# An output product in split precision, loads reordered, and three stage starts prepared by the stage ahead

## The reference

```python
def mixer_sublayer(x, mem, w_in, w_mem_kv, w_out, main_fn):
    h = x @ w_in
    ...
    y_main = main_fn(u_main)
    y_mem = memory_attention(q_mem, mem, w_mem_kv)
    y = jnp.concatenate([y_main * jax.nn.silu(g_main), y_mem * jax.nn.silu(g_mem)], axis=-1)
    return y @ w_out
...
        x = layer_norm(ALPHA * x + y, ln_g[layer], ln_b[layer])
...
        y_a = _gmlp_mixer(zu, zv, ...)
        y_b = _rwkv7_mixer(zr, ...)
        y = jnp.concatenate([y_a, y_b], axis=-1) @ w_out[l]
        x = x + gate1[:, None, :] * y
        h = _modulate(_rmsnorm(x, norm2_g[l]), shift2, scale2)
        y = _hier_moe(h, router_group_w[l], router_group_b[l], router_expert_w[l],
                      router_expert_b[l], moe_w_gate[l], moe_w_up[l], moe_w_down[l])
```

## Time and profile before

| | |
|---|---|
| Median of 3 runs | 3203.99 us (3201.82 to 3207.22) |
| The profiled execution | 3200.6 us, span of the trace 3198.9 us |
| Granted TensorE clock, mean | 0.942 |
| TensorE busy | 2877.6 us, 90% of the span |
| VectorE, ScalarE, GpSimd busy | 1745.5, 1076.3, 440.4 us |
| Second output stage | 1410.6 to about 1601 us |
| Mixing stage | 2189.1 to 2455.7 us |

### The profile page before, as it was taken

The page is one execution under the profiler, slowest core; times in us unless marked ns, Lnnn a source line. Parts: engine busy times, 40 slices in busy tenths (PEclk is TensorE's granted clock), DMA queues, the critical chain, the costliest instruction groups (busy, mean ns, idle before and its releaser), DMA issues. The chain is left out here.

```text
span 3198.9 us, 46062 instructions
## 1 busy us (share of the span) xinstructions
PE 2877.6 (90%) x18692; PEld 2100.5 (66%) x18692; DVE 1745.5 (55%) x2741; ACT 1076.3 (34%) x1682; POOL 440.4 (14%) x352
## 2 busy tenths in 40 slices
PE   7999899898999999989889999995796799999991
PEld 5877644576777777754436767684675577777770
DVE  2223323484565666633324625352674799999984
ACT  2111100122444444531221313221243366666652
POOL 1322000021332222300021101011200000000001
PEclk9999999999999999989999999996697799999995
DMA  4111031563212112121121201017433799999985
GB/s 155 50 37 42 7 132 53 182 202 106 66 54 60 53 54 60 54 112 46 40 58 30 67 26 58 7 59 242 144 114 145 254 397 398 398 396 398 399 305 223
DMA packets 290854, 454.34 MB, mean 142 GB/s; under 512 B 15680, under 2 KB 157504, under 8 KB 290672
## 3 DMA queue, kind: packets, MB, share of 16 engines
q1 hardware_dynamic: 283616, 426.05, 38.0%
q0 software_dynamic: 7056, 25.69, 2.0%
HBM read 389.77 MB, written 61.93 MB: 141 GB/s over the span
## 5 line engine op out<-in xcount | busy, mean ns | idle before, releaser
L662 PE MATMUL psum<-wo,yT 128*128 128x512 f32 x768 | 336.3, 598 | 14.6 <-DMA wo<-in_w_out 14.6
L662 PEld LDWEIGHTS psum<-wo,yT 128*128 128x128 f32 x768 | 146.5, 192 | 195.1 <-issue 179.5
L922 PE MATMUL psum<-x_hi,w_hi 128*128 128x512 f32 x512 | 211.4, 413 | 10.2 <-POOL w_lo L1023 10.2
L1112 DVE TENSOR_TENSOR fox_pT_lo<-psum,fox_pT_hi 128x512 fp32r<-128x512 f32 (+2 forms) x192 | 107.1, 558 | 184.8 <-ACT fox_pT_hi L1051 175.7
L924 PE MATMUL psum<-x_hi,w_lo 128*128 128x512 f32 x512 | 201.7, 394 | 0.0
L923 PE MATMUL psum<-x_lo,w_hi 128*128 128x512 f32 x512 | 200.7, 392 | 0.0
L2874 ACT CAST hi_d<-land_d 128x2048 fp32r<-128x2048 f32 x66 | 122.8, 1909 | 140.1 <-PE psum L2746 140.1
L1603 PE MATMUL psum<-hT,wr 128*128 128x512 f32 x384 | 167.1, 593 | 0.0
L162 PE MATMUL psum<-x_hi,w_hi 128*128 128x512 f32 x384 | 152.7, 398 | 9.0 <-POOL w_lo L153 9.0
L3019 DVE TENSOR_TENSOR lo_d<-land_d,hi_d 128x2048 fp32r<-128x2048 f32 x66 | 148.3, 2289 | 21.5 <-ACT hi_d L2874 21.5
L164 PE MATMUL psum<-x_hi,w_lo 128*128 128x512 f32 x384 | 151.2, 394 | 0.0
(11 more groups left out here) (493 smaller groups left out, 6498.4 us busy)
## 6 DMA issues: line engine op xcount, KB each, us to landing
land_g<-in_moe_w_gate SPq DMA_DIRECT2D x66, 1024.0 KB, 7.6
land_u<-in_moe_w_up SPq DMA_DIRECT2D x66, 1024.0 KB, 7.2
land_d<-in_moe_w_down SPq DMA_DIRECT2D x66, 1024.0 KB, 9.0
ada<-in_ada_w SPq DMA_DIRECT2D x24, 1024.0 KB, 5.4
y_slots<-yb SPq DMA_DIRECT2D x33, 512.0 KB, 10.0
w<-in_w_in SPq DMA_DIRECT2D x24, 512.0 KB
wo<-in_w_out SPq DMA_DIRECT2D x12, 1024.0 KB
w_land<-in_w_in SPq DMA_DIRECT2D x24, 512.0 KB, 3.8
```

Of the source, the lines that this page charges most:

```text
L662: last = nc.tensor.matmul(banks[hf][:], E.yT[:, c, t * P:(t + 1) * P], wo[:, c, hf * HALF:(hf + 1) * HALF], start=(c == 0), stop=(c == NY ...
L922: nc.tensor.matmul(bank[:], hi[:, d, :], E.x_hi[:, d, cols], start=(d == 0), stop=False)
```

## The change

Six parts.

1. `stage_out` gets a parameter `whole`. In layer 1 it is 2: chunks 0 and 1 stay f32 matmuls, chunks 2 to 11 become three f32r matmuls each. ScalarE casts ten chunks of w_out, VectorE subtracts them; for each tile GpSimd casts and subtracts y (128x1280). `wo_lo` and `y_lo` take the place of `wo` and `yT` in memory. Two x tiles instead of three. Layer 0 keeps f32.
2. The first two key blocks of the memory stage of layer 1 are loaded by SyncE at the end of layer 0's `stage_out`, into tiles that both stages share. The memory stage in turn loads and splits the first q and the first k block of the fox stage at its end, behind the last `ada` load. `stage_fox` starts with `FIRST = 2` blocks present.
3. In `tail(c)` of the RWKV stage `fill_("GH", c)` moves from behind both heads' GH to between the two, on TensorE and on ScalarE. The four router loads move into this stage's start, waited for at its end.
4. The mixing stage loads by first use; the waits for small operands are split up; the transposes of `ws` follow the first two chains; the zeros are written in five parts, issued in the steps t = 8 to 12 behind the stores of these steps.
5. The casts of `w_o` go from GpSimd to ScalarE, in step t = 2 in front of the copies of tile 0's y; GpSimd keeps the eight subtractions.
6. In the routing preamble the eight small operations for the two weights move behind the first block's `e_x_lo`; TensorE makes the first eight of the table's products when the first choice is placed; two subtractions of expert weights move in front of the wait for the table.

```diff
-def stage_out(nc, E, A, layer, rows_in, rows_out, modulate=False):
+def stage_out(nc, E, A, layer, rows_in, rows_out, modulate=False, whole=NY):
...
+        SPLIT = NY - whole
+        with ExitStack() as raw:
+            wo = E.sb("wo" + n, [P, NY, D], ctx=raw)
+        wo_lo = E.sb("wo_lo" + n, [P, NY, D], F32R, ctx=st)
+        if SPLIT:
+            wo_hi = E.sb("wo_hi" + n, [P, SPLIT, D], F32R, ctx=st)
+            y_hi = [E.sb(f"y_hi{n}_{i}", [P, SPLIT, P], F32R, ctx=st) for i in range(2)]
...
-        NX = 3
+        NX = 2 if SPLIT else 3
...
+                        if t == 0 and c >= whole:
+                            pe.wait_ge(wo_split, c - whole + 1)
+                        if c == whole:
+                            pe.wait_ge(y_split, t + 1)
...
+                            if c < whole:
+                                last = nc.tensor.matmul(banks[hf][:], E.yT[:, c, t * P:(t + 1) * P], wo[:, c, cols], start=first, stop=final)
+                            else:
+                                hi, w_hi = y_hi[t % 2][:, c - whole, :], wo_hi[:, c - whole, cols]
+                                nc.tensor.matmul(banks[hf][:], hi, w_hi, start=first, stop=False)
+                                nc.tensor.matmul(banks[hf][:], hi, wo_lo[:, c, cols], start=False, stop=False)
+                                last = nc.tensor.matmul(banks[hf][:], E.y_lo[:, c, t * P:(t + 1) * P], w_hi, start=False, stop=final)
...
+                if layer == 0:
+                    wkv = A["w_mem_kv"][1].rearrange("(c p) n -> p c n", p=P)
+                    for i in range(2):
+                        sp.dma_start(E.w1[i][:], wkv[:, :, i * P:(i + 1) * P]).then_inc(E.w1_landed[i], 16)
...
+            def _(pool):
+                for t in range(NT if SPLIT else 0):
+                    cols = slice(t * P, (t + 1) * P)
+                    if t >= 2:
+                        pool.wait_ge(ringD.full, ringD.nth(("y", t - 2, 1)))
+                    nc.gpsimd.tensor_copy(y_hi[t % 2][:], E.yT[:, whole:NY, cols]).then_inc(y_hi_set, 1)
+                    pool.wait_ge(y_hi_set, t + 1)
+                    nc.gpsimd.tensor_tensor(E.y_lo[:, whole:NY, cols], E.yT[:, whole:NY, cols], y_hi[t % 2][:].bitcast(F32),
+                                            ALU.subtract).then_inc(y_split, 1)
...
+                for c in range(whole, NY):
+                    if c % 2 == 0 or c == whole:
+                        act.wait_ge(wo_landed[c // 2], 16)
+                    nc.scalar.copy(wo_hi[:, c - whole, :], wo[:, c, :]).then_inc(wo_hi_set, 1)
...
+                for c in range(whole, NY):
+                    dve.wait_ge(wo_hi_set, c - whole + 1)
+                    nc.vector.tensor_tensor(wo_lo[:, c, :], wo[:, c, :], wo_hi[:, c - whole, :].bitcast(F32), ALU.subtract).then_inc(wo_split, 1)
...
-                        pe.wait_ge(w_split, m + 1)
+                        if m >= FIRST:
+                            pe.wait_ge(w_split, m - FIRST + 1)
...
-                for m in range(2):
-                    load_w(m)
                 for j in range(2):
                     load_ncum(j)
-                for m in range(2, len(loads)):
+                for m in range(FIRST, len(loads)):
...
+        ahead = [("fox_q", 0), ("fox_k", 0)]
...
+                for m in range(len(order), len(order + ahead)):
+                    load(m)
...
+                        if j == 1:
+                            fill_("GH", c)
...
-                    fill_("GH", c)
...
+                sp.dma_start(E.rw[:, :, 0:N_GROUPS], A["router_group_w_2"][0].rearrange("(c p) n -> p c n", p=P)).then_inc(router_landed, 16)
+                sp.dma_start(E.rw[:, :, N_GROUPS:], A["router_expert_w_2"][0].rearrange("(c p) n -> p c n", p=P)).then_inc(router_landed, 16)
+                sp.dma_start(E.rb[:, 0:N_GROUPS], A["router_group_b_2"].broadcast_to([P, N_GROUPS])).then_inc(router_landed, 16)
+                sp.dma_start(E.rb[:, N_GROUPS:], A["router_expert_b_2"].broadcast_to([P, EXPERTS])).then_inc(router_landed, 16)
...
+                for x in ("n", "mt", "uv"):
+                    load(x, 0)
+                sp.dma_start(ws[:], A["gmlp_ws_2"][0].rearrange("h t s -> t h s")).then_inc(w_landed["ws"], 16)
+                rows(ln_w, "gmlp_ln_w_2", "ln")
+                rows(ln_b, "gmlp_ln_b_2", "ln")
+                load("qt", 0)
+                for x in ("n", "mt", "uv"):
+                    load(x, 1)
+                sp.dma_start(bs[:], A["gmlp_bs_cols"]).then_inc(small, 16)
+                sp.dma_start(g2[:], A["rwkv_g2_2"][0]).then_inc(small, 16)
+                load("yi", 0)
+                load("v", 0)
+                rows(gn_w, "rwkv_gn_w_2", "gn")
+                rows(gn_b, "rwkv_gn_b_2", "gn")
+                for x in ("qt", "yi", "v"):
+                    load(x, 1)
+                sp.dma_start(w_o[:], A["w_out_2"][0].rearrange("(c p) n -> p c n", p=P)).then_inc(w_landed["o"], 16)
+                sp.dma_start(gate[:], E.gates[:, 0:D]).then_inc(w_landed["gate"], 16)
+                for t in range(NX):
                     load_x(t)
-                sp.dma_start(w_o[:], A["w_out_2"][0].rearrange("(c p) n -> p c n", p=P)).then_inc(w_landed["o"], 16)
-                sp.wait_ge(zeros_set, 1)
...
+                    if t >= NT:
+                        part = slice((t - NT) * ZEROS, (t - NT + 1) * ZEROS)
+                        sp.dma_start(further[:, part, :], zeros[:].rearrange("p (o n) -> p o n", o=1).broadcast_to([P, ZEROS, ZW])).then_inc(zeroed, 16)
...
-                    nc.gpsimd.tensor_copy(w_o_hi[:, d, :], w_o[:, d, :]).then_inc(wo_hi_set, 1)
...
+                    if t == 2:
+                        act.wait_ge(w_landed["o"], 16)
+                        for d in range(ND):
+                            nc.scalar.copy(w_o_hi[:, d, :], w_o[:, d, :]).then_inc(wo_hi_set, 1)
...
-                pe.wait_ge(R["places"], 1)
                 for n in range(TOP_K * NT):
                     k, t = n // NT, n % NT
+                    if t == 0:
+                        pe.wait_ge(R["places"], k + 1)
...
+                lo("g0", 0)
+                lo("g1", 0)
                 dve.wait_ge(R["table"], 1)
...
-                for x in UP_PIECES[0:3]:
-                    lo(x, 0)
+                lo("u0", 0)
                 modulate(M, 0, 0)
                 lo_x(M, 0, 0)
+                link(dve, V.tensor_reduce(den[:], gexp[:], X, ALU.add))
+                link(dve, V.reciprocal(den[:], den[:]))
```

More of the change, by code:

```diff
@@ L1245, in load @@
                 def load(m):
-                    kind, h = order[m]
+                    kind, h = (order + ahead)[m]
                     if m >= NW:
                         used(sp, m - NW)
-                    if kind in "kv":
+                    if kind == "fox_q":
+                        src = win[:, :, 0:P]
+                    elif kind == "fox_k":
+                        src = A["w_kv_shared"].rearrange("(c p) n -> p c n", p=P)[:, :, 0:P]
+                    elif kind in "kv":
                         src = wkv[:, :, (h + (MEM_HEADS if kind == "v" else 0)) * P:(h + 1 + (MEM_HEADS if kind == "v" else 0)) * P]
@@ L1254, in load @@
                     sp.dma_start(w[m % NW][:], src).then_inc(landed[m % NW], 16)
-                for m in range(2):
-                    load(m)
                 forget.load(sp)
@@ L1283, in _ @@
                 forget.split(pool)
-                for m in range(KV, len(order)):
+                for m in range(KV, len(order + ahead)):
                     k = m - KV
@@ L2184, in stage_mix @@
         zeros, zeros_set, zeroed = sb("zeros", [P, ZW]), E.sem("zeros_set"), E.sem("slots_zeroed")
-        w_landed = {x: E.sem("mix_" + x) for x in ("o", "ws", "row")}
+        further = y_slots[EXPERTS * P:SLOTS, :].rearrange("(p b) d -> p (b d)", p=P).rearrange("p (k n) -> p k n", n=ZW)
+        ZEROS = OVER * D // ZW // 5
+        w_landed = {x: E.sem("mix_" + x) for x in ("o", "ws", "ln", "gn", "gate")}
         x_landed = [E.sem(f"x2_landed{i}") for i in range(NX)]
@@ L2273, in router, with turn_ws @@
                     for d in range(ND):
-                        last = nc.tensor.matmul(bank[:, 0:NR], h2T[t % 2][:, d, :], rw[:, d, :], start=(d == 0), stop=(d == ND - 1))
+                        last = nc.tensor.matmul(bank[:, 0:NR], h2T[t % 2][:, d, :], E.rw[:, d, :], start=(d == 0), stop=(d == ND - 1))
                     last.then_inc(ringD.full, 1)
-                pe.wait_ge(sems["tril"], 1)
-                for h in range(2):
-                    bank = take(ringA, ("ws", h))
-                    for k in range(4):
-                        last = nc.tensor.transpose(bank[:, k * P:(k + 1) * P], ws[:, 4 * h + k, :], E.ident[:])
-                    last.then_inc(ringA.full, 1)
-                pe.wait_ge(small, 16 * 6)
+                def turn_ws():
+                    pe.wait_ge(sems["tril"], 1)
+                    for h in range(2):
```

(23 more changed lines are left out.)

119 lines of the change are left out of this document (60 added, 59 removed).

## The result

The changed kernel takes 3159.4 us (median of 4 runs, 3157.9 to 3163.4) against 3205.6: ratio 0.9861, 95% interval 0.9848 to 0.9875. That is 46 us less; 58 were forecast, and the range of 3127 to 3167 holds it. The profiled execution has a span of 3156.9 us against 3198.9, 42.0 less, and the traces tell where they are. A stage is counted here from its first DMA issue to that of the next one.

A forecast was written before the change was run, and what follows sets the result against it. TensorE, busy for 90% of the span, was taken to bound the kernel. Terms of 24.6, 3.5, 10.4, 1, 12 and 6.7 us sum to 58.2, giving a median of 3146 us from 3204.0; range 3127 to 3167.

The forecast's parts named there:

- Output stage: Output stage of layer 1: ten of twelve chunks as f32r matmuls shorten a tile to 18.3 us; -24.6 us, ends 22 and 27.
- Fox: Start of the fox stage: first two blocks split beforehand, clock stays at full speed; -10.4 us, ends 8 and 11.
- Memory stage: Memory stage of layer 1: earlier loads remove the 6.3 us wait, about 2 us come back; -3.5 us, ends 0 and 4.1.
- RWKV: RWKV stage: GH filling moved between the two halves hides a 3.27 us wait; -1 us, ends -4 and +1.
- what TensorE gains in front of that wait is lost in it: RWKV stage: time gained before TensorE's later 1.54 us wait for VectorE goes into that wait, since VectorE's chain ignores GH.
- the clause on the fox stage: Fox stage: the clock fell to 0.50 after 9 us of idleness; with under 2 us it stays full, saving 1.9 us.
- Mixing: Mixing stage: new load order, less the cost of w_out's split and the zeros; sum -14.5, taken as -12 us, ends -24 and 0.
- A stall of over 10 us: Mixing stage: such a stall for the streams of tile 2 would make the sum wrong; a wait under 5 us was expected.
- the -26: Mixing stage: with loads reordered and zeros later, the streams of tile 2 land near 2224 instead of 2250; -26 us.
- Rival 1: Mixing stage: each of eight subtractions locks VectorE out for its 2.39 us, so nothing is gained; 3158 us, chance 0.18.
- Experts: Experts' preamble: small operations moved, half the table's products run early, two subtractions moved forward; -6.7 us, ends 4.5 and 8.
- Together 6.7: Experts' preamble: the sum of 1.7 from small operations, 3.5 from the table's products and 1.5 from the subtractions.

The follow-up runs named there:

- edit 7: The changed kernel with the output product of layer 1 back in plain f32 (all twelve chunks whole, three x tiles): 3184.3 us, ratio 0.9951.

## Why the prediction was right, and where it wasn't

- **Output stage: right**, a little too small. -24.6 forecast with ends of 22 and 27, -27.9 measured, and edit 7 gives all of it back. A tile is 17.96 us, not 18.3, and tile 0, from TensorE's first matmul to tile 1's, took 19.9 us where it had been 22.8. That GpSimd's split hides was right: it takes 10.0 + 23.1 us for eight tiles, 4.1 per tile for the 4.3 of the forecast.
- **Fox: right**, -11.6 for -10.4. The first matmul starts 0.05 us into the stage instead of 7.4, and the clock stayed up, as forecast. No run undid this part; the trace alone shows it.
- **Memory stage: right in size** as far as it can be told, -2.5 over several traces for -3.5; the one trace of before hid it.
- **RWKV: wrong**, +10.9 for -1 with a range of -4 to +1. The step that failed is "what TensorE gains in front of that wait is lost in it". Its sum of waits was nearly right for the move alone (+1.4 us), less so in the changed kernel (+4.1). What the step left out is the clock: it treated a pause moved from one place to another as the same pause, though the clause on the fox stage, some lines above, priced the clock behind a pause. On the kernel before, the move cost 5.7 us in the stage, 4.2 of them clock. The rest of the stage's loss, some 5 us between single traces, was in no term and isn't explained by these runs.
- **Mixing: right in its large parts.** The streams let VectorE start tile 2 24.9 us earlier (63.3 us into the stage before, 38.5 after) for 26. With the locks VectorE took 24.2 us from tile 2's T to tile 3's, where it had been 17.7: +6.5 for +6. The other subtractions made 28.1 of 25.9 from there to tile 4's T: +2.2 for +3. The end: +3.9 for +2.5. Another 3.1 us, from tile 7's T to the last store (75.1 for 71.9), are in no term; kernels alike in this code gave 71.9 to 76.6 there, so no edit need be behind them. The wait left for the streams, 12.5 us, was said to be under 5: the streams took longer from the moment VectorE was ready, since tiles 0 and 1 were done at 2190, 31 us into the stage and not 32, and the streams landed at 37, not 35. A stall of over 10 us there was named as a sign that the sum is wrong, and it came. It was a poor sign: the -26 is counted on VectorE, which waited only 7.8 us. Rival 1, every subtraction a full lock on the path, would have given 0; -9.3 lies nearer the forecast. The rule of the Trainium skill, "SBUF — State Buffer", section "Who interferes with whom", names the mechanism: of VectorE with two SBUF inputs and GpSimd, the one that comes second blocks for the other's whole instruction, and an operation with an input from PSUM doesn't. These traces agree, with 2.73 us and 0.69.
- **Experts: half**, -3.3 for -6.7 with ends of 4.5 and 8. The indices came 4.2 us earlier for 5.2, and from the transposes to the first expert matmul it is 6.2 us instead of 8.8, 2.6 less for 1.5. But the gather took 8.5 us instead of 4.5 and ate 4 of that: the first expert matmul is 2.8 us earlier. The step that failed is the sum "Together 6.7", which left the gather's time as it was. Freeing land_g early, by the two subtractions moved forward, let the next 2 MB start in front of it.

The total came out in the range since the two errors are of 12 and 3.4 us against a width of 40, and the output stage gave 3 more than its term. That is the width's doing and no merit of the RWKV term. The measured 3159 lies next to rival 1's 3158, by coincidence: rival 1 has the mixing stage gain nothing, and it gained 9.3 us; the time was lost in another stage.

## What to carry to other kernels

Where a piece of work is moved into a pause, find the next instruction on that engine that another engine's chain releases: here the pause came back there, and what followed it ran in part at half clock; move a second piece there, or leave both. GpSimd's two-input work beside VectorE's two-input work cost VectorE the whole GpSimd instruction here (2.73 us for 0.69), so put it in VectorE's own stall, on VectorE, where it took 9.2 us instead of 19.8. When a buffer is freed earlier, ask which transfer that starts and what small transfer it will overtake.

## What the runs showed of the hardware

- The gather of 128 rows took 4.5 to 4.75 us with no load ahead of it (the DMA moved 152 to 154 GB/s in that time) and 8.5 us when a load of 2 MB had been issued 2.6 us ahead (351 GB/s).
- In the second output stage VectorE's TENSOR_SCALAR of 1024 columns with one input tile in SBUF took 1.51 us on average while GpSimd split y, and 0.81 with GpSimd idle, in the kernel before and in edit 7; the two-input operations of 1024 columns there took 1.23 as before, because they came later: at the first tile GpSimd's subtraction ended at 1427.60, the TENSOR_SCALAR ran from 1426.42 to 1428.15, and the first two-input operation began at 1428.18. All of it lay beside TensorE's tile:

```profile
L780 DVE TENSOR_SCALAR x_tile<-x_tile,ln_mv,ln_rstd 128x1024 f32<-128x1024 f32 x8 | 12.1, 1509 | 0.3
```

- The kernel before, unchanged, took 3194 to 3209 us in 13 runs of one session. A difference of 5 us between single traces of two kernels is not yet one between the kernels; the average over several traces told more about the memory stage than one could.
